# Two norms ahead of the second attention folded into one factor per token, applied to each product of the stage

## The reference

```
def rmsnorm(x, g):      # at the end of the first block, g = final_g
    inv = rsqrt(mean(x * x, axis=-1) + 1e-6);  return (x * inv) * g

# second block
h = rmsnorm_2(x, norm_mix_g)            # x is the result of the norm above
z = h @ w_in                            # 1024 x 7184
uv = gelu(z[..., :2048]);  z_u, z_v = uv[..., :1024], uv[..., 1024:]
q, k, v = z[..., 2048:3072], z[..., 3072:4096], z[..., 4096:5120]
f_logit = z[..., 5120:5136];  gates = sigmoid(z[..., 5136:])
a = z_u * (W_s layernorm(z_v) + b_s)    # per block of 128 tokens and group of 128 columns
b = softmax(q k / 8 + running sums of log_sigmoid(f_logit + b_f), causal) v    # 16 heads
x = x + (gate_a * (a @ w_branch_a) + gate_b * (b @ w_branch_b)) @ w_out
```

## Time and profile before

| | us |
|---|---|
| median of 3 runs | 2216.02 |
| lowest, highest | 2214.74, 2218.69 |
| profiled execution, its own time | 2216.38 |
| its span, first to last instruction | 2214.6 |
| PE busy | 2089.1 (94%) |
| DVE busy | 1306.8 (59%) |
| ACT busy | 860.9 (39%) |
| mean granted TensorE clock | 0.967 |

### The profile page before, as it was taken

How to read it: one execution, slowest core, us unless ns; L and a number is a source line. 1 busy time by engine, 2 the same in 40 slices (tenths; PEclk the granted TensorE clock), 3 DMA queues, 4 the chain that set the end, 5 groups by cost and what they waited for, 6 DMA issues and landing times.

```text
span 2214.6 us, 28642 instructions
## 1 busy us (share of the span) xinstructions
PE 2089.1 (94%) x9417; PEld 1724.1 (78%) x9417; DVE 1306.8 (59%) x1573; ACT 860.9 (39%) x1228; POOL 310.6 (14%) x222
## 2 busy tenths in 40 slices
PE   2999999999999989999995999998999999999997
PEld 2788888787788878888883788877788888888876
DVE  6777577578654453333346666668433577547765
ACT  2332223377433333222233565563322344334443
POOL 0789997000000000000000000012000000000000
PEclk6999999899999989999997999999999999999999
DMA  7466664321233323233322222234333323333232
GB/s 275 142 190 181 196 194 141 96 67 57 62 87 98 104 58 104 85 93 106 88 77 72 67 59 74 66 67 95 86 95 95 95 86 95 90 100 102 78 99 73
DMA packets 371706, 226.81 MB, mean 102 GB/s; under 512 B 8053, under 2 KB 361673, under 8 KB 370633
## 3 DMA queue, kind: packets, MB, share of 16 engines
q1 hardware_dynamic: 362248, 193.66, 29.7%
q0 software_dynamic: 9408, 32.51, 5.3%
HBM read 224.05 MB, written 2.10 MB: 102 GB/s over the span
## 4 chain that ended last, share of the span: by engine, by line
PE 88%; DVE 7%; ACT 3%; issue 2%; DMA 0%; DVEq 0%; POOL 0%; ACTq 0%
PE ps L451 27%; PE ps L452 27%; PE ps L453 27%; PE ps L539 1%; PE ps L562 1%; DVE x L1437 1%; PE ps L550 1%; PE ps L577 1%; PE ps L578 1%; PE ps L551 1%; DVE wl L1223 1%; DVE x L1427 1%; DVE ssq L1236 1%; DVE ada_acc L1605 0%; PE ps L492 0%
## 5 line engine op out<-in xcount | busy, mean ns | idle before, releaser
L451 PE MATMUL ps<-uh,wh 128*128 128x512 f32 x1896 | 749.6, 395 | 18.7 <-DVE ul L1270 7.8
L452 PE MATMUL ps<-ul,wh 128*128 128x512 f32 x1896 | 743.1, 392 | 0.0
L453 PE MATMUL ps<-uh,wl 128*128 128x512 f32 x1896 | 743.1, 392 | 0.0
L1223 DVE TENSOR_TENSOR wl<-raw,wh 128x1024 fp32r<-128x1024 f32 x389 | 546.5, 1407 | 225.5 <-ACT wh L837 219.4
L837 ACT ACTIVATE wh<-raw 128x1024 fp32r<-128x1024 f32 x389 | 408.7, 1052 | 210.6 <-PE ps L453 200.5
L451 PEld LDWEIGHTS ps<-uh,wh 128*128 128x128 f32 x1896 | 359.5, 190 | 96.4 <-issue 21.5
L453 PEld LDWEIGHTS ps<-uh,wl 128*128 128x128 f32 x1896 | 358.7, 189 | 76.0
L452 PEld LDWEIGHTS ps<-ul,wh 128*128 128x128 f32 x1896 | 359.5, 190 | 73.7 <-issue 0.5
L451 PE MATMUL ps<-ah,wh 128*128 128x512 f32 x528 | 208.6, 395 | 0.0
L453 PE MATMUL ps<-ah,wl 128*128 128x512 f32 x528 | 208.5, 395 | 0.0
L452 PE MATMUL ps<-al,wh 128*128 128x512 f32 x528 | 208.4, 395 | 0.0
(11 more groups left out here) (250 smaller groups left out, 2233.2 us busy)
## 6 DMA issues: line engine op xcount, KB each, us to landing
raw<-in_ffn_w_gu SPq DMA_DIRECT2D x88, 512.0 KB, 4.2
raw<-in_w_in SPq DMA_DIRECT2D x57, 512.0 KB, 3.8
ada_ring<-in_w_ada POOLq DMA_DIRECT2D x56, 512.0 KB, 4.1
raw<-in_w_up SPq DMA_DIRECT2D x44, 512.0 KB, 3.8
raw<-in_w_mix_in SPq DMA_DIRECT2D x40, 512.0 KB, 3.8
raw<-in_ffn_w_down SPq DMA_DIRECT2D x32, 384.0 KB, 3.2
raw<-in_ffn_w_down SPq DMA_DIRECT2D x32, 320.0 KB, 2.9
wada<-in_w_ada SPq DMA_DIRECT2D x8, 1024.0 KB, 12.7
```

What stands on the lines that cost most here:

```text
L451: pe.matmul(dst, lh, rh, start=first, stop=False, skip_group_check=True)
L452: pe.matmul(dst, lh, rl, start=False, stop=False, skip_group_check=True)
L453: return pe.matmul(dst, ll, rh, start=False, stop=last, skip_group_check=True)
L1223: dve.tensor_tensor(wl[:, w], raw[:, w], wh[:, w].bitcast(F32), ALU.subtract).then_inc(w_lo, 1)
```

## The change

The second norm acts on the first one's result, so both together multiply a token by one number. If ms1 is the mean of h squared and ms2 the mean of (final_g h) squared, that number is 1 / sqrt(ms2 + eps ms1 + eps eps). The `eps ms1` part is put into the weights of the second sum: ACT squares `h` once more with a per-channel scale sqrt(final_g squared + eps) (`square_weighted`), DVE sums it (`add_weighted`). `uh` and `ul` become `h` times final_g times norm_mix_g, written in `ffn2`'s last loop (`scaled_hi`, `scaled_lo`). PE makes both means in the middle of the first pair of chunks (`both_means`). Each of the stage's products (32 of the attention, 8 of the gating stage, 16 gates of `merge2`, and the forget gates) is multiplied in PSUM by the factor `inv12` (`scale`), and every reader waits for that. `h` itself, which the residual needs, is multiplied by `final_g` and `inv1` inside the attention, one tile in each round. The first F product moves ahead of the first scores, into another bank. ACT copies F at the end of a round instead of at the start of the next, and turns head 0's probabilities out before it writes the next weights. In the gating stage `normal_group`'s first step goes from DVE to ACT (`normal_rows`), and its tables lie in three slots instead of four.

```diff
@@ tensor @@
+            def both_means():
+                pe.wait_ge(ssq2_add, 10)
+                pe.matmul(bank(B_MEAN12), mean_w[:, :], ssq2[:, :], start=True, stop=True).then_inc(ms_done, 1)
+                pe.wait_ge(ssq_add, 9 * 3 + 10)
+                pe.matmul(bank(B_MEAN1), mean_w[:, :], ssq[:, :], start=True, stop=True).then_inc(ms_done, 1)
...
-                    dense_pair(nb - 1, (B_HEAD[1], B_O), DT, uh, ul, u_at(norm))
+                    dense_pair(nb - 1, (B_FG, B_O), DT, uh, ul, u_at(norm), both_means)
                     dense(nb + 1, 0, B_DENSE, DT, uh, ul)
-                dense(nb + 2, 0, B_V, DT, uh, ul)
-                first_scores(0)
-                dense(nb + 3, 0, B_DENSE, DT, uh, ul)
+                    dense(nb + 2, 0, B_V, DT, uh, ul)
+                    dense(nb + 3, 0, B_F0, DT, uh, ul)
+                    first_scores(0)
+                    pe.wait_ge(A_["f"], 1)
...
             ffn("ffn2", False)
-            mean_square(3)
-            mean_square(4)
@@ scalar @@
+            def square_weighted(m, r):
+                act.wait_ge(ssq2_add, m + 1)
+                act.activation(sq2[:, r * S:(r + 1) * S], tile(h, m), ACT.Square, scale=gains[:, bass.ds(m + GN_ROOT, 1)]).then_inc(sq2_done, 1)
...
+                def result(n, c, it):
+                    if kind == 1:
+                        done(c, it)
+                    else:
+                        act.wait_ge(scaled, it + (n + 1))
                 def q_hi(c, it):
-                    done(c, it)
+                    result(c - nb, c, it)
...
                 def body(p, last):
                     it = 4 * p
-                    f_out(nb + 3, it, p)
                     split(nb + 3 + LEAD, it)
                     soft(p, 1)
...
                     if not last:
                         q_hi(nb + 4, it)
-                        split(nb + 4 + LEAD, it)
...
                     turned_hi(p, 0)
+                    if not last:
+                        split(nb + 4 + LEAD, it)
...
                     act.activation(tile(t["oh"], p), sq[:, S:2 * S], ACT.Copy).then_inc(A_["o_hi"], 1)
+                    if not last:
+                        f_out(nb + 7, it, p + 1)
...
-            ffn("ffn2", False)
-            root(3)
-            with act.Fori(0, DT // 2) as i:
-                for r in range(2):
-                    square_tile(4, 2 * i + r, r)
-            norm(4, 3, None)
+            ffn("ffn2", False, (3, gains, GN_MIX))
+            root(3, rt, B_MEAN12, eps2_col)
+            root(4, rt1, B_MEAN1)
...
+            def normal_rows(m):
+                if m == 0:
+                    act.wait_ge(G["rinv"], 2)
+                act.wait_ge(G["v_lo"], m + 1)
+                for b in range(ST):
+                    x = act.activation(sq[:, b * P:(b + 1) * P], vtok[:, b * D + m * P:b * D + (m + 1) * P], ACT.Identity,
+                                       scale=rstd[:, b:b + 1], bias=nmr[:, b:b + 1])
+                x.then_inc(G["n1"], 1)
@@ vector @@
+            def scale(b, by):
+                dve.tensor_tensor(bank(b), bank(b), by[:, :], ALU.mult).then_inc(scaled, 1)
...
                             if part == 1:
                                 add_square(q, 2 * i + r, r)
+                                if f == "ffn2":
+                                    add_weighted(2 * i + r, r)
...
+                def result(n, b, it):
+                    if kind == 2:
+                        done(nb + n, it)
+                        scale(b, inv12)
                 def body(p, last):
...
                     if not last:
+                        result(4, B_O, it)
                         q_lo(p + 1)
                     turned_lo(p, 0)
...
                     if not last:
                         split(nb + 4 + LEAD, it)
+                    if kind == 2:
+                        dve.scalar_tensor_tensor(tile(h, p), tile(h, p), cols[:, bass.ds(p + C_FIN, 1)], inv1[:, :], ALU.mult, ALU.mult)
                     if not last:
+                        result(5, B_DENSE, it)
                         k_lo(p + 1)
                         split(nb + 5 + LEAD, it)
...
                     turned_lo(p, 1)
                     if not last:
+                        result(6, B_V, it)
                         split(nb + 6 + LEAD, it)
...
                     dve.tensor_tensor(tile(t["ol"], p), sq[:, S:2 * S], tile(t["oh"], p).bitcast(F32), ALU.subtract).then_inc(A_["o_lo"], 1)
+                    if not last:
+                        result(7, B_DENSE, it)
...
+                result(0, B_O, 0)
+                if kind == 2:
+                    inverse(4, inv1, rt1)
                 q_lo(0)
                 if kind == 2:
                     forget_sums()
                 split(nb + LEAD, 0)
+                result(1, B_DENSE, 0)
                 k_lo(0)
                 split(nb + 1 + LEAD, 0)
+                result(2, B_V, 0)
                 split(nb + 2 + LEAD, 0)
+                result(3, B_F0, 0)
                 v_lo(0)
...
-            ffn("ffn2", False, (small, M_G2))
-            inverse(3)
-            clear_sum(4)
-            for k in range(DT):
-                dve.scalar_tensor_tensor(h[:, k * S:(k + 1) * S], h[:, k * S:(k + 1) * S], cols[:, C_FIN + k:C_FIN + k + 1],
-                                         inv[:, :], ALU.mult, ALU.mult).then_inc(h_new, 1)
-            for k in range(DT):
-                add_square(4, k, k % 2)
-            norm(4, 3, (cols, C_NMIX), None)
+            ffn("ffn2", False, (small, M_G2), (3, gains, GN_MIX))
+            inverse(3, inv12, rt)
...
+            for m in range(2):
+                done(AT_["zu"] + m, 0)
+                scale(m, inv12)
             dve.wait_ge(G["vg"], ST + 1)
...
                 dve.tensor_tensor(tile(gal, m), sq[:, S:2 * S], tile(gah, m).bitcast(F32), ALU.subtract).then_inc(G["a_lo"], 1)
+                if m + 2 < DT:
+                    done(nb + m + 2, 0)
+                    scale(m % 2, inv12)
```

## The result

| | before | changed |
|---|---|---|
| median, us | 2215.89 | 2231.61 |
| lowest, highest (4 runs each) | 2214.74, 2218.69 | 2230.52, 2231.75 |
| span of the profiled execution | 2214.6 | 2229.8 |
| PE, DVE, ACT busy | 2089.1, 1306.8, 860.9 | 2104.1, 1321.9, 874.8 |

The changed kernel is slower: ratio 1.0068, interval 1.0051 to 1.0085. The forecast was 2220.0, in a range of 2208 to 2234. So the sign that I held likeliest came, but with 15.7 us where the forecast had 4, and with the size that I gave to a rival (2231.6).

The account below looks back on a forecast made before the run. The prediction took PE to bound the loop before, and a DVE-ACT chain after. Start -27.8, rounds +27.5, last round +0.5, gating +3.2, set-up +0.2 sum to +3.6 on 2216.4: 2220.0 us, range 2208 to 2234.

Parts of the forecast that it names:

- the sign that I held likeliest: Whole kernel: slower, meaning over 2220.4 us, given 0.48 against 0.35 for same and 0.17 for faster.
- What bounds the kernel: PE idles in the norms' stretch, which can be won; the attention's loop is full on PE, with 1.4 to 1.5 slack.
- my first rival: Attention's loop: work added to DVE costs nothing since PE is fuller; round stays 30.95, 2192 us; 10%.
- The start: From `ffn2` to the attention's loop: the loop starts at 1222.7 instead of 1250.5, -27.8 us.
- The round: Attention's loop: a chain through DVE and ACT makes rounds 34.6 instead of 30.95 us; seven rounds lose 27.5.
- the walk: One loop round traced with each operation started once engine and input are there: 31.0 us before, 34.6 changed.
- The gating stage: Start +1.8, eight groups +1.4 (8.3 us for each of six, 6.1 for the last step): together +3.2 us.
- The rest: `merge2`, the first attention and `ffn2`'s last loop: 0 each; set-up +0.2 us.
- All is under PE: Attention's loop: DVE's added work fits beneath PE's, so the round stays 30.95; 2192 us; 10%.
- part of it fits: Attention's loop: each scaling costs only its 0.7 us, 2.8 a round, 19.6 in seven; 2212 us; 13%.
- The start stays late: Ahead of the loop or in its first round: half of the 27.8 us gain missing, 2234 and more; 7%.
- The rival of the clock: Attention's loop: two short PE waits lower the array's clock, up to 1.7 us a round, 11.6 in seven; 2231.6; 20%.

Follow-up runs that it names:

- run 1: The changed kernel with the four multiplications by the factor left out of each round of the second attention's loop: 2198.47 us.
- run 2: The changed kernel with Q's multiplication alone left out of the loop's rounds: 2212.99 us.
- run 3: The changed kernel with V's multiplication alone left out of the loop's rounds: 2220.65 us.
- run 5: The changed kernel with K's multiplication alone left out of the loop's rounds: 2213.83 us.
- Run 7: The changed kernel with the gating stage's normalising step back on DVE instead of ACT: 2235.04 us.
- run 6: The changed kernel with ACT again writing the second-next weights' high part ahead of head 0's turned probabilities: 2236.18 us.
- run 8: The changed kernel with four needless matmuls in each loop round ahead of PE's wait for head 1's low probabilities: 2230.27 us.

## Why the prediction was right, and where not

- **What bounds the kernel** held. The norms' gap was there to be won and the loop had no room. The slack of 1.4 to 1.5 us decided, not the busy share. The Trainium skill, "Perfetto Trace Analysis", section "Identifying the Most-Contended Engine", has one take the engine with the highest occupancy as the most contended and optimize it first. In the trace that is PE, before and after; it does not follow that work added to DVE is free, as my first rival had it: DVE, at 68% before and after, costs 3.92 a round when it gets 2.8 more multiplying to do, and PE gives up 20 of 252 us.
- **The start** was right to 0.4 (predicted 1222.7 for the loop's first row, found 1223.07), in part by luck: `ffn2` ended 1.35 later than before (1186.48 for 1185.13; 1185.41 in the second profile of the changed kernel), and from its last matmul to the loop 36.6 us passed where the prediction has 37.6.
- **The round** was right as a mechanism: three waits of 0.75, 1.38 and 0.86 where 0.9, 1.8 and 0.8 were given, and runs 1, 2, 3 and 5 take each multiplication's part away as the walk has it. Its length was 0.34 too short, which with the first round makes 2.2 of the 7.3 us that the seven rounds were off. It lies in the third wait: from head 1's first values to the scores 1286.82 - 1284.26 = 2.56 us pass (2.53 to 2.56 in every round), where 1.27 passed before. So PE loses 1.3 there and not 0.8; the 0.89 in the bracket counts only from the end of the last matmul's row, which the next one would have overlapped. The loops that keep V's multiplication run 0.3 to 0.5 over the walk, those without it at most 0.2.
- **The clock** is the other 5.2: 251.50 less 36.45 and six times 34.98. I had this as a rival for the whole difference, at up to 1.7 in every round (seven times 1.7 are 11.9 and not its 11.6). What happens is rarer and can be larger: three of seven rounds are longer, by 0.5, 1.6 and 3.0. From the scores' first matmul to the next product 3.71 and 3.99 us pass where the array goes down, and 2.14 in the other rounds. The step that failed is the sum of the forecast, which took nothing for it although the walk has two waits close ahead of the scores. The Trainium skill, "TensorE: Matmul & The Clock Gate", section "HAM oscillation — how this bites in real kernels", describes an array that goes cold in each turn of a loop with a long wait for a DMA in it. Here the trace agrees in that the array runs at a granted clock of 0.50 behind waits inside a loop, at waits of 1.39 and 0.89, but not in each turn; why in these turns stays open.
- **The gating stage** was mis-sized: +5.6 for +3.2. Its start is right (+2.1 for +1.8), and PE waits for a table of POOL only once there, 3.72 us for 4.42 before. But ACT's four normalising operations take 1.64 us (DVE's took 1.12), where I had let them take about 0.95. So they come out of the low weights' cover, DVE waits 0.37 for them, and the groups stand 8.63 to 8.77 apart and not 8.3, 2.2 us in six; the last step takes 6.6 for 6.1. Run 7 shows that the move was right nevertheless.
- **The rest** has +1.3 instead of 0. No run shows it to be the change's: from `merge2` to the end the changed kernel and the runs that have its code there take 652.0 to 654.7 us, and the granted clock over `merge2`'s first 10 us is 0.73 in the changed kernel, 0.83 before and 1.00 in run 6.
- **The rivals.** "All is under PE" and "part of it fits" were wrong by run 1: the multiplications cost 3.92 a common round, not 0 and not 2.8. "The start stays late" was wrong by the trace. The rival of the clock gave 2231.6 and the median is 2231.61, but only 5.2 of its 11.6 us come from the clock; the rest is the round, the gating stage and small terms. That the total of that rival came to the median is chance: a total that agrees does not prove its sum.

## What to carry to other kernels

An engine that is 68% busy can have no room: look at how long before its reader starts each result is out, and walk one round through with the new operations in their places. To apply a per-token factor to every product instead of once to the operand trades one wait ahead of a stage for an operation in every round; where the stage's loop has a chain through that engine, fold the arithmetic but apply it once (here 2199.9 against 2231.6 us). Prices taken by leaving out one operation at a time overlap (2.26 + 2.10 for two, 3.92 for all four).

## What the runs showed of the hardware

- Behind two waits of PE of 1.39 and 0.89 us with 1.7 us of matmuls between them the granted clock was 0.50 in some rounds; behind the same pair it was 1.00 in others, and in run 6 behind 1.31 and 0.86 in each round. Behind 1.38 alone (run 3) or 0.86 to 0.89 alone (runs 2 and 8) no round of the profiled loops had it. Behind one wait of 2 us a matmul took 0.47 in one kernel and 0.77 in another, and behind one of 2.9 the next 10 us had a granted clock of 0.73 in one execution and of 1.00 in another.
- With four needless matmuls in a wait the loop of the profiled execution was 5.1 us shorter; the medians show no clear gain.
- Four operations of 128x128 with a scale and a bias per partition take 1.64 us on ACT and 1.11 on DVE.
